# One weight place, one contiguous piece: re-laying the buffers of a two-layer hybrid backbone with a streamed mixture of experts

## The reference

```python
for g in range(N_GROUPS):            # 4 groups of 8 experts, two experts per token
    gate_w = (group_mask[:, g:g + 1] * expert_w).astype(t.dtype)
    hid = jax.nn.silu(jnp.einsum('td,edf->tef', t, p['moe_w_gate'][g])) * jnp.einsum('td,edf->tef', t, p['moe_w_up'][g])
    out = out + jnp.einsum('tef,efd->td', hid * gate_w[..., None], p['moe_w_down'][g])
```

## Time and profile before

| | |
|---|---|
| median of 3 runs | 1373.34 us (1372.44 to 1374.03) |
| the profiled execution, its own time | 1372.54 us |
| its span in the trace | 1370.7 us |
| TensorE busy | 1208.6 us, 88% of the span |
| VectorE busy | 602.7 us, 44% |
| ScalarE busy | 305.9 us, 22% |
| moved by DMA | 321.43 MB, mean 234 GB/s |
| mean granted TensorE clock | 0.928 |

### The profile page before, as it was taken

How to read it: one execution, slowest core, us unless ns; L and a number is a source line. 1 busy time by engine, 2 the same in 40 slices (tenths; PEclk the granted TensorE clock), 3 DMA queues, 4 the chain that set the end, 5 groups by cost and what they waited for, 6 DMA issues and landing times. The chain is left out here.

```text
span 1370.7 us, 19955 instructions
## 1 busy us (share of the span) xinstructions
PE 1208.6 (88%) x7788; PEld 796.7 (58%) x7788; DVE 602.7 (44%) x1217; ACT 305.9 (22%) x623; POOL 133.3 (10%) x144
## 2 busy tenths in 40 slices
PE   6799998999899989998877789998789889988783
PEld 3544546987678864554544466457667745555451
DVE  4432985136973541342111355954284533322223
ACT  4202112254543201131011232122442200000001
POOL 0000000000000012222121100000000112322210
PEclk9899999998989989999898899999999889999997
DMA  8643133245651579999999745342473869999992
GB/s 280 198 145 123 62 108 93 65 135 187 226 181 37 211 263 367 394 385 358 383 374 376 282 149 172 104 124 73 140 256 136 343 263 386 372 379 384 384 369 114
DMA packets 162550, 321.43 MB, mean 234 GB/s; under 512 B 30009, under 2 KB 113014, under 8 KB 144792
## 3 DMA queue, kind: packets, MB, share of 16 engines
q1 hardware_dynamic: 150968, 304.08, 62.3%
q0 software_dynamic: 11392, 15.79, 3.5%
q10 hardware_dynamic: 96, 0.26, 0.0%
HBM read 320.32 MB, written 21.23 MB: 249 GB/s over the span
## 5 line engine op out<-in xcount | busy, mean ns | idle before, releaser
L660 PE MATMUL bank<-hT,ring 128*128 128x512 f32 (+1 forms) x544 | 208.6, 542 | 1.8 <-DVE hT L1784 1.8
L660 PE MATMUL bank<-ring,hT 128*128 128x256 f32 (+1 forms) x928 | 184.6, 354 | 4.2 <-ACT hT L1401 1.7
L660 PEld LDWEIGHTS bank<-ring,hT 128*128 128x128 f32 x928 | 157.4, 197 | 25.2 <-issue 3.5
L660 PEld LDWEIGHTS bank<-hT,ring 128*128 128x128 f32 x544 | 105.1, 196 | 99.1 <-issue 91.4
L1788 DVE TENSOR_TENSOR xbc<-xbc,bank 64x256 f32<-64x256 f32 x65 | 27.5, 423 | 291.0 <-ACT xbc L1401 229.4
L660 PE MATMUL bank<-ring,qkT 128*64 128x256 f32 x608 | 107.4, 412 | 8.7 <-DMA ring<-in_moe_w_up 4.7
L1401 ACT ACTIVATE xbc<-bank 64x256 f32<-64x256 f32 x65 | 24.5, 378 | 356.9 <-PE bank L660 356.8
L1334 POOL DMA_INDIRECT pair_rows<-hyT,zotok x65 | 65.5, 1008 | 395.9 <-ACT hyT L1401 202.0
L660 PEld LDWEIGHTS bank<-ring,qkT 128*64 128x64 f32 x608 | 65.1, 148 | 24.9 <-issue 8.2
L660 PE MATMUL bank<-hT,qkT 128*64 128x256 f32 x288 | 67.5, 419 | 12.0 <-DMA ring<-in_moe_w_up 8.2
L1401 ACT ACT_TABLE_LOAD x33 | 42.3, 1283 | 126.0 <-PE bank L660 74.1
(11 more groups left out here) (344 smaller groups left out, 1930.9 us busy)
## 6 DMA issues: line engine op xcount, KB each, us to landing
ring<-in_w_mod SPq DMA_DIRECT2D x40, 1024.0 KB, 7.7
ring<-in_w_in SPq DMA_DIRECT2D x22, 1024.0 KB, 5.7
ring<-in_moe_w_up SPq DMA_DIRECT2D x22, 1024.0 KB, 20.1
ring<-in_moe_w_down SPq DMA_DIRECT2D x18, 1024.0 KB, 16.4
ring<-in_moe_w_gate SPq DMA_DIRECT2D x16, 1024.0 KB, 17.7
hT<-in_moe_w_gate SPq DMA_DIRECT2D x12, 1024.0 KB, 19.9
xtok<-in_moe_w_gate SPq DMA_DIRECT2D x11, 1024.0 KB, 11.3
zotok<-in_moe_w_up SPq DMA_DIRECT2D x11, 1024.0 KB, 13.5
```

The lines of the kernel that those rows point to most:

```text
L660: return nc.tensor.matmul(o, a, b, start=s, stop=e, **k)
```

## The change

All buffers that are free during the mixture of experts are laid side by side, so that each place is one area of 2048 columns. `hfilt`, `xbc`, `zotok`, `state`, `vaug` and `hsum` become slices of one buffer `chain`; `dft`, `inv`, `keep` and `wgr` become slices of `tables`; `spare` goes, and `big` grows from 9 to 12 blocks of 512 columns. There are 18 places instead of 19. One half of `tabs_v` moves from `xbc` to `hyT`, and `hid_v`, `hidT_v`, the router's tables and `also` move to `ktok` and `ysum`.

```diff
-ONCE = ((8, 9, 18, 10, 15, 16, 14), (11, 12, 8, 9, 13, 10, 15, 16, 17, 14))
+ONCE = ((8, 17, 9, 13, 10, 16, 15, 14), (11, 8, 17, 9, 12, 13, 10, 16, 15, 14))
...
-PLACES = 19
+PLACES = 18
...
-    return s < MOE_SLOTS or s >= 14 or (n <= LAST_IN_TAPS if l == 0 else s in (8, 9, 10, 11))
+    return l > 0 or s not in (8, 10) or n <= LAST_IN_TAPS
...
+        tables = sb("tables", 2048)
+        dft, inv, keep, wgr = (tables[:, 512 * n:512 * n + 512] for n in range(4))
+        chain = sb("chain", 12288)
+        hfilt, xbc, zotok = chain[:, 0:2560], chain[:, 2560:5120], chain[:, 5120:8192]
+        state, vaug, hsum = chain[:, 8192:8972], chain[:, 8972:10532], chain[:, 10532:12068]
...
-        big = sb("big", 9 * 512)
+        big = sb("big", 12 * 512)
...
-        hid_v = xbc[:, 0:2 * EH].rearrange("p (u n) -> p u n", u=2)
+        hid_v = ktok[:, 1024:1024 + 2 * EH].rearrange("p (u n) -> p u n", u=2)
...
-            (qkT[:, 1024:3072],), (xbc[:, 1536:2560], vaug[:, 0:1024]), (hsum[:, 0:1024], hyT[:, 2048:3072]),
-            (x[:, 0:2048],), (spare[:, 0:1024], dft[:, :], inv[:, :]),
-            (hfilt[:, 1024:2048], spare[:, 1024:1536], keep[:, :]),
-            (big[:, 2048:4096],), (hyT[:, 1024:2048], vaug[:, 1024:1536], hsum[:, 1024:1536]),
-            (state[:, 0:512], zotok[:, 512:1024], xbc[:, 1024:1536], hfilt[:, 2048:2560]),
-            (big[:, 4096:4608], wgr[:, :], hfilt[:, 512:1024], grow[:, 0:512]), (spare[:, :], big[:, 4096:4608])]
+            (qkT[:, 1024:3072],), (chain[:, 8192:10240],), (hyT[:, 1024:3072],), (x[:, 0:2048],), (tables[:, :],),
+            (chain[:, 4096:6144],), (big[:, 2048:4096],), (chain[:, 10240:12288],), (chain[:, 2048:4096],),
+            (big[:, 4096:6144],)]
...
                     sp.wait_ge(*due(("xn", l, 1, 1)))
                     expert(first.index(11))
-                    sp.wait_ge(*due(("made", ("yt", l, 1, 1))))
-                    expert(first.index(12))
...
-                    if s in (8, 9, 13, 18):
+                    if s in (8, 9, 12, 17):
                         sp.wait_ge(*due(("made", ("mn", l, 2 * NT - 1))))
-                    elif s == 6:
+                    elif s in (6, 13):
...
-                    elif s in (10, 15, 16, 17):
+                    elif s in (10, 15, 16):
```

More of the change, by code:

```diff
@@ L56 @@
 RELOADED = (6, 7, 0, 1, 2, 3, 4, 5)
-ONCE = ((8, 9, 18, 10, 15, 16, 14), (11, 12, 8, 9, 13, 10, 15, 16, 17, 14))
-FIRST_ORDER = ((8, 9, 18, 6, 7, 0, 1, 2, 3, 10, 15, 16, 4, 5, 14), (11, 12, 8, 9, 6, 13, 7, 0, 1, 2, 3, 10, 15, 16, 17, 4, 5, 14))
-PLACES = 19
+ONCE = ((8, 17, 9, 13, 10, 16, 15, 14), (11, 8, 17, 9, 12, 13, 10, 16, 15, 14))
+FIRST_ORDER = ((8, 17, 9, 6, 13, 7, 0, 1, 2, 3, 10, 16, 15, 4, 5, 14), (11, 8, 17, 9, 12, 6, 13, 7, 0, 1, 2, 3, 10, 16, 15, 4, 5, 14))
+PLACES = 18
 MOST_PAIRS = 2 * NT * P
@@ L224, in build @@
         gcolp = sb("gcolp", 4)
-        wgr = sb("wgr", KB * 64)
         gsel = sb("gsel", 2 * P)
@@ L307, in build @@
         taps_v = qkT[:, 1024:3072].rearrange("p (t e o c) -> p t e o c", t=2, e=2, o=2)
-        tabs_v = [a.rearrange("p (e o c) -> p e o c", e=2, o=2) for a in (xbc[:, 1536:2560], hyT[:, 2048:3072])]
+        tabs_v = [a.rearrange("p (e o c) -> p e o c", e=2, o=2) for a in (hyT[:, 1024:2048], hyT[:, 2048:3072])]
         hid_a, hid_b, hid_c = (ysum[:, 256 * r:256 * r + 256] for r in range(3))
@@ L333, in build @@
         item_hot = qkT[:, 0:2 * NT * 2 * ITEMS].rearrange("p (n v i) -> p n v i", n=2 * NT, v=2)
-        weight_of = ztok[:, 0:48]
-        token_of, pair_of = ztok[:, 64:64 + 48].bitcast(U32), ztok[:, 128:128 + 48].bitcast(U32)
-        more_expert, more_flag = ztok[:, 192:192 + MORE_ITEMS].bitcast(I32), ztok[:, 208:209].bitcast(I32)
+        weight_of = ysum[:, 1216:1264]
+        token_of, pair_of = ysum[:, 1280:1328].bitcast(U32), ysum[:, 1344:1392].bitcast(U32)
+        more_expert, more_flag = ysum[:, 1408:1408 + MORE_ITEMS].bitcast(I32), ysum[:, 1424:1425].bitcast(I32)
         rows_v = big[:, 0:2048].rearrange("p (u d) -> p u d", u=2)
         rowsT_v = qkT[:, 0:2 * KB * ITEM_ROWS].rearrange("p (u k n) -> p u k n", u=2, k=KB)
-        hid_v = xbc[:, 0:2 * EH].rearrange("p (u n) -> p u n", u=2)
-        hidT_v = xbc[:, 512:512 + 4 * ITEM_ROWS].rearrange("p (u f n) -> p u f n", u=2, f=2)
+        hid_v = ktok[:, 1024:1024 + 2 * EH].rearrange("p (u n) -> p u n", u=2)
+        hidT_v = ysum[:, 768:768 + 4 * ITEM_ROWS].rearrange("p (u f n) -> p u f n", u=2, f=2)
         res_v = hyT[:, 0:D].rearrange("p (u n) -> p u n", u=2)
@@ L571, in _ @@
                     fetch(f"route{l}_in", dst, A["const_" + name])
-                for s in FIRST_ORDER[l][2 if l else 0:]:
-                    if s in (8, 9, 13, 18):
+                for s in FIRST_ORDER[l][1 if l else 0:]:
+                    if s in (8, 9, 12, 17):
                         sp.wait_ge(*due(("made", ("mn", l, 2 * NT - 1))))
-                    elif s == 6:
+                    elif s in (6, 13):
                         sp.wait_ge(*due(("gated", l, MIX_ORDER[l][-1])))
@@ L2481, in _ @@
                 each = ysum[:, 0:MORE_ITEMS * 32].rearrange("p (j e) -> p j e", j=MORE_ITEMS)
-                also = room(MORE_ITEMS * 32).rearrange("p (j e) -> p j e", j=MORE_ITEMS)
+                also = ysum[:, 480:480 + MORE_ITEMS * 32].rearrange("p (j e) -> p j e", j=MORE_ITEMS)
                 numbers = iota[:, 0:MORE_ITEMS].unsqueeze(2).broadcast_to([P, MORE_ITEMS, 32])
```

10 lines of the change are left out of this document (removed).

## The result

The changed kernel takes 1359.26 us in the median of 4 runs (1357.35 to 1360.48), and the kernel before, measured beside it, 1372.89 us in 4 runs (1370.39 to 1374.03). The ratio is 0.9902, with a 95% interval of 0.9884 to 0.992. The gain is 13.6 us where 10.6 had been forecast, and the time lies inside the range of 1355 to 1369 us. The profiled execution took 1357.35 us, 15.2 less than that of before.

A forecast was written before the change was run, and what follows sets the result against it. The stream of weights was taken to bound both mixtures of experts. Layer 0's 5.7 us and layer 1's 4.9 us make 10.6 off the profiled 1372.54 us; with 0.8 added for the median, 1362.7 us, range 1355 to 1369 us.

The forecast's parts named there:

- The bound: In both mixtures of experts the stream of weights sets the end, with TensorE waiting for matrices.
- Fewer packets: Recycled loads of both layers: 90 fewer areas at 0.04 us each, 1.7 us in layer 0 and 1.9 in layer 1.
- The rival of dearer packets: Cut rows cost more in the full stream: 0.11 us an area, 10 us instead of 3.6, giving 1356.3 us; chance 0.12.
- Layer 1's start: Loads ahead of layer 1's items end earlier, so the first gather's wait goes: 3.0 us, bounds 0 and 3.0.
- Layer 0's matrix ahead: Layer 0: place 13 loaded ahead leaves 83 matrices instead of 84 behind the large hole: 2.8 us, bounds 0 and 2.8.
- the small hole: Layer 0, no load issued from 533.54 to 540.90 us: refilling place 13 removes it, 1.2 us, bounds 0 and 1.2.
- the large hole: Layer 0's pause in loads until 503.14 us, waiting for item 0 to free matrices; forecast to stay.
- the wait at 746.47 us: Layer 0: TensorE waits 3.03 us for an `up` matrix, read as showing that the layer's end hangs on the stream.
- More places in layer 1: Layer 1: eighteen places circulate instead of sixteen, but the stream is already full after the first items: 0 us.
- Free packets: Rival: only matrix ahead, hole and layer 1's earlier start remain, 1366.3 us, or 1369 if one fails; chance 0.22.
- TensorE didn't become the bound: Rival: with fewer waits TensorE would be full to the end; judged not to decide, no chance given.
- Late gathers: Rival: gathers land late behind more queued bytes, 0.3 us for each of 65 items, giving 1382 us; chance 0.05.

The follow-up runs named there:

- halves: Changed kernel with every place from 8 on loaded as two areas of 1024 columns, 75 recycled areas more: 1365.68 us, 0.9947, 7.6 +-3.9 us slower than the changed kernel.
- quarters everywhere: Changed kernel with every place from 8 on loaded as four areas of 512 columns, 225 recycled areas more: 1376.95 us, 1.003, 18.9 +-3.5 us slower.
- the 80 areas: Changed kernel with places 15, 16 and 17 cut as before, 80 recycled areas more: 1370.2 us, 0.9985, 12.8 +-3.3 us slower than the changed kernel.
- the old schedule uncut: Changed kernel's buffers with the schedule of before (place 12 of layer 1 in the mn group), every place loaded whole: 1365.84 us, 0.995 of the kernel before.
- one matrix back: Changed kernel with layer 1's place 17 loaded behind place 15 again, where it was before: 1363.43 us, 0.9924, 4.4 +-4.0 us slower than the changed kernel.
- the kernel of the blocks: Changed kernel with places from 8 on loaded by four DMAs of 32 neighbouring partitions, whole rows: 1583.55 us, 1.1495, 220 us slower than the changed kernel.
- the repetition: The changed kernel run again, unedited, as the base of the comparisons: 1358.02 us, 0.9892 of the kernel before.

## Why the prediction was right, and where its terms were off

**The bound.** It was rightly read as the stream of weights. Further packets lengthened the part of layer 1 behind item 2's transpose in every trace with cut areas (229.7 to 235.9 us, against 228.1 to 229.1 with whole rows), and TensorE still idles for 19 of 200 us in layer 1 and for 23 in layer 0.

**Fewer packets: right mechanism, mis-sized.** I took 0.04 us for an area, 3.6 us in all, with bounds of 0.029 and 0.069. Measured are 8.1 +-3.3 us for these 90 areas and the 22 of the first fills (0.09 for each of the 90), 0.10 for halves, 0.084 for quarters everywhere and 0.16 +-0.04 for the 80 areas; the queue's engine time gives 0.11 from before to after. So the price of 0.04 was less than half of what was measured. The upper bound of 0.069 lies inside the intervals of the first two and at the edge of the third, and below that of the fourth; its 8.7 ns is below the 13 to 16 ns of every pair of kernels. The step that failed is the choice "so I stay near it", with the two short stretches of layer 1. They lie ahead of the items, with three gathers in all, and 8 and 11 us are short for a difference of 2%. By the weight queue's engine time the same two stretches would have said something else: it is busy for 100.4% of the first (461 packets, 3.38 MB) and 103.9% of the second (1613 packets, 4.50 MB), that is 38.0 and 40.6 engine-us for a MB, or an estimate of 11.8 ns for each of the 222 further packets. The rival of dearer packets had a price nearer to this (0.11 us), and the loss does appear in the full stream (381 and 392 GB/s with and without cuts, at a share of 1.02); its sum of 1356.3 us was 3.0 too low, the forecast's 3.4 too high. The Trainium skill, "DMA: Bandwidth & Descriptors", section Specifications, would have a row of 512 bytes or more at line rate and so a price of nothing; the runs disagree with it by 8.1 +-3.3 us.

**Layer 1's start: right in kind, about half of what was measured.** Forecast were 3.0 us and a transpose 4.5 us behind its gather. It is 4.80, which is 2.9 us less than before, so the wait was sized well. But up to item 2's transpose the gain is 5.8 us. The step left out what TensorE does after the wait. In the three traces shown above, item 0 takes 5.16 us with no wait for the rows (the changed kernel), 6.47 behind a wait of 2.73 us (the old schedule uncut) and 8.09 behind one of 2.90 (one matrix back). The windows over item 0 show why. In the changed kernel:

```profile
1091.80:1097.00 5.20, 4.98 (x43) 3.11 (x43) 3.80 (x8) 0.00 (x0) 0.00 (x0) 1.00 0.03 6
```

in the old schedule uncut:

```profile
1097.60:1104.00 6.40, 6.35 (x42) 3.74 (x42) 3.80 (x8) 0.00 (x0) 0.00 (x0) 0.73 0.00 0
```

and with one matrix back:

```profile
1091.00:1099.00 8.00, 8.00 (x42) 4.63 (x42) 3.79 (x8) 0.00 (x0) 0.00 (x0) 0.57 0.00 0
```

It is the same 42 or 43 matmuls each time, and the granted clock is 1.00, 0.73 and 0.57: behind the wait a part of the item, in the last the larger part, runs at the lower level, and TensorE is busy 4.98, 6.35 and 8.00 us for it. Where item 0 pays less, item 1 pays the rest. Its windows, in the changed kernel and in the old schedule uncut:

```profile
1096.90:1103.80 6.90, 4.79 (x45) 3.55 (x43) 1.40 (x3) 1.66 (x2) 0.00 (x0) 1.00 0.73 281
...
1104.10:1112.60 8.50, 6.39 (x44) 4.53 (x42) 1.40 (x3) 1.66 (x2) 0.00 (x0) 0.80 0.66 247
```

Items 0 and 1 together take 12.0 us in all six traces in which item 0 waits for its rows for 0.3 us or less, 13.7 us in the three with a wait of 0.97 to 1.63 us, and 14.8 to 15.0 us in the four with a wait of 2.73 to 3.32 us, leaving aside the kernel of the blocks. So the lower clock behind the wait of before cost as much again as the wait, 3.0 us (14.96 against 12.0). The cause of the wait itself is shown: one matrix issued later brings it back without a packet more.

**Layer 0's matrix ahead and the small hole: most likely far too large.** 2.8 + 1.2 = 4.0 us were forecast. The kernel without either is +0.4 +-3.7 us, the two sets of traces differ by 0.7 us, and closing the hole altogether gives nothing measurable. Two steps failed. The hole was costed at its old place, "I take the whole hole", and in the changed kernel a hole of the same share lies ten microseconds earlier. And a matrix less behind the large hole does end the stream some 6 us earlier in one pair of traces, but TensorE ends the layer hardly earlier. I took the wait at 746.47 us as proof that the end hangs on the stream; the changed kernel has such a wait too, on TensorE's timeline:

```profile
749.36 0.40 PE L649 MATMUL bank<-hT,qkT 128*64 128x256 f32 x1 [1.78 <-DMA ring<-in_moe_w_up]
```

A wait in one item tells that this item was late; by itself it doesn't tell that the layer's end follows the stream byte for byte. That TensorE's last items then set the end fits the traces, but no run isolates it.

**More places in layer 1: forecast 0, measured about 0.6 us** in the traces, with the same rate of the full stream (392 and 393 GB/s). No run with this part alone was made, so the size rests on one trace with sixteen whole places against seven with eighteen.

**The sum.** Of the 10.6 us, 4.0 were layer 0's schedule, 3.6 the packets and 3.0 layer 1's start. The runs give 0.4 for the first, 8.1 for the second, 5.5 for the third (22.3 against 16.8 us, both uncut) and 0.6 for layer 1's places: 14.6 us, where 13.6 and, in the repetition, 14.8 were measured. The first two have intervals of 3 to 4 us and the others come from single traces, so that the sum meets the measured gain is no proof of its parts. Two terms were too low (by 4.5 and 2.5 us) and one too high (by 3.6), and partly cancelled. That the forecast came within 3.4 us is in this part luck.

**The rivals.** Free packets fall by the cut kernels. TensorE didn't become the bound. Late gathers would have shown as waits for rows. The view of waits has, for TensorE in the whole kernel (us, number, longest), before

```profile
PE bank L1214 <- DMA big<-h_rows,zotok: 6.9, 6, 3.0
```

and after

```profile
PE bank L1203 <- DMA big<-h_rows,ysum: 6.5, 5, 2.1
```

so the waits are no more and no longer in sum. They have moved: layer 1's first is gone, and layer 0's first grew from 0.95 to 2.15 us.

**What stays open.** Why the 225 areas of the quarters cost less for each than the 80 of the first cut kernel (0.084 against 0.16, with intervals that don't meet), and why the kernel with neither place 13 nor 9 handed on is slower than both its neighbours. A part of the first is seen: all three kernels with the changed order and cut areas lose 2.4 to 3.0 us at layer 1's start, whatever their number of recycled areas. Open are also the earlier first gather of layer 0, and which side of a DMA the blocks of 32 rows burden. No kernel tried is faster than the changed one.

## What to carry to other kernels

When a kernel is bound by a DMA stream, price a packet by the queue's engine time over whole spans of two kernels that differ in nothing else, and don't take it from short quiet stretches: here each further packet cost 13 to 16 ns on an engine, whether its row was cut in halves or in quarters. Look first at what is queued ahead of the first gather, since one megabyte, loaded in a later group, delayed layer 1 by 5.4 us in the trace (4.4 +-4.0 in the time), twice the time that it takes to move. When you cost a wait of TensorE, look at the granted clock of the work behind it too: here this doubled the price of a wait of 3 us. And ask of each hole in a stream whether anything at the far end waits for it; the small one of layer 0, in plain view here, gave nothing measurable when it was closed.

## What the runs showed of the hardware

With each matrix loaded by four DMAs of 32 neighbouring partitions (and so 32 neighbouring rows of the matrix), the full stream moved 276 GB/s; with four DMAs of every fourth partition and row it moved 378 GB/s, at the same number and size of DMAs and the same share of 1.02. That was the largest effect of all runs, 220 us. The number of DMAs by itself cost nothing measurable (225 more, +1.4 +-4.2 us).

In the steady stream of the changed kernel SyncE's issues are themselves blocked, as its timeline in layer 1 shows:

```profile
1259.49 2.77 SPq L543 DMA_DIRECT2D x<-in_moe_w_up  x1
1262.31 0.44 SPq L543 DMA_DIRECT2D tables<-in_moe_w_down  x1
1262.80 7.22 SPq L543 DMA_DIRECT2D chain<-in_moe_w_gate  x1
1270.06 2.32 SPq L543 DMA_DIRECT2D chain<-in_moe_w_up  x1
```

An issue that takes 0.33 us at 1097.63 us, when the queue is short, takes up to 7.22 us here. The DMA share from 1110 to 1310 us is 1.02, so this isn't a loss. The long time is that of the issue itself and not of a wait ahead of it. This suggests that more loads stand in the queue than it can hold, which no run tests.
